# The first eight modulation parts in places of their own, and the filter network of layer 0 in another order

## The chip, the cores and the metric

The kernel runs on one NeuronCore of one Trainium2 chip. Five engines work beside each other and meet at semaphores: TensorE (matmuls, and the loads of their stationary operand), VectorE, ScalarE, GpSimd, and SyncE (SP), which here only issues DMAs. The metric is the device time of one execution in microseconds; smaller is better.

## What is computed

Two layers of a backbone over 256 latent tokens and 256 context tokens, width 1024, in float32. Cut to what the change touches:

```
for i in range(2):
    mod_l = split(silu(c)     @ w_mod[i] + b_mod[i], 6)       # w_mod[i]: 1024 x 6144
    mod_c = split(silu(c_ctx) @ w_mod[i] + b_mod[i], 6)
    uc = modulated_norm(xc, norm1_w, mod_c[0], mod_c[1]) @ w_in[i]
    ul = modulated_norm(xl, norm1_w, mod_l[0], mod_l[1]) @ w_in[i]
    ...                                                        # SSD, Hyena, mLSTM mixers, then 32 experts

modulated_norm(x, w, shift, scale) = rmsnorm(x, w) * (1 + scale) + shift

def hyena_filters(L, p):                                       # depends on weights alone
    hdn = sin(freq * (feats @ w1 + b1))
    hdn = sin(freq * (hdn @ w2 + b2))
    return (hdn @ w3).reshape(L, 2, 2, 256) * exp(-t * abs(decay))

def bidir_long_conv(z, h_fwd, h_bwd):
    two_sided = [h_fwd, 0, reversed h_bwd[1:]]
    two_sided = two_sided / sum(abs(two_sided))                # the "tap sum", one value per channel
    return irfft(rfft(z) * rfft(two_sided))
```

The input projection needs the modulated norm, and that needs vectors 0 (shift) and 1 (scale) of the modulation, each 1024 wide: the first 2048 columns of `w_mod`. The filter's spectra are needed later, in the Hyena mixer.

## The kernel before

**Modulation parts.** `w_mod` is taken in parts of 256 columns, 1 MB each in float32. Parts 0 to 3 give vector 0, parts 4 to 7 vector 1. Part n is loaded by `modulation(0, n)` on SP into one of the four slots of `ring` (2048 columns each), in rows of a kilobyte; TensorE multiplies it in eight matmuls of 256 columns that are spread over the four 32-column groups of the array; ScalarE copies the product to `grow` (`mod_rows`). When a vector's four parts are there, TensorE adds up the groups and turns the result into columns (`mod_vector`, 16 matmuls with `four`), and VectorE adds the bias (`mod_columns`). With eight parts and four slots, parts 4 to 7 wait until parts 0 to 3 are used.

**Filter network** (`filter_step`, one function on each of TensorE, ScalarE and VectorE). Step 0 and 1: a hidden layer each; VectorE brings the argument of the sine into range, ScalarE does the sine. Step 2: the taps, four matmuls of 512 columns, times the decay window. Step 3: ScalarE writes the absolute values to `tabs_v` (parts of `xbc` and `hyT`), TensorE sums them over the rows by 16 matmuls with one column each (`tapsum`), then VectorE makes sum and difference of the two directions (with a copy of each difference) and the reciprocal. Step 4: five spectra, two matmuls of 512 columns each, copied to `hfilt` by VectorE.

**Order at the start.** Each engine runs its instructions in the order of the code, and the order is written out by hand, per engine: lines 399 to 432 for SP, 614 to 648 for TensorE, 1243 to 1275 for ScalarE, 1564 to 1688 for VectorE. SP's queue is filled in this order: condition vectors, parts 0 and 1, filter parameters, parts 2 and 3, x, the DFT tables, biases and norm weights, parts 4 to 7, the layer's parameters and other constants, then the projection's weights alternating with further parts. TensorE ends the stretch with 32 transposes of the normed x; ScalarE (context) and VectorE (latent) write them to `hT` with the modulation applied; `stage_end` is a meeting of TensorE, ScalarE and VectorE. The input projection follows.

**Layer 1** has the same filter network. Its steps are placed between the experts of layer 0, at the items in `FILTER_ITEMS`; item j's three weight matrices stream through eight slots of 1 MB.

**Names.** Every matmul is recorded at line 533, every ScalarE instruction at 1208, VectorE's at 1540 to 1550, by helpers. A float32 matmul stands in the trace as two passes, so 8 matmuls are x16 (a transpose is one). PSUM has eight banks in turn (`product`).

## Time and profile before

| | us |
|---|---|
| median of 3 runs | 1513.99 |
| lowest and highest of them | 1511.68, 1515.15 |
| the profiled execution | 1514.76 |
| its span, on which all times of the trace lie | 1512.8 |
| TensorE busy in the span | 1242.1 (82%) |
| VectorE, ScalarE busy | 633.8, 315.8 |
| HBM traffic over the span | 226 GB/s |

Times of rows are in microseconds from the start of the span unless marked ns. A row of a timeline is: start, length, engine, line, operation, what is written `<-` what is read, shapes, count, and in brackets how long the engine was idle before it and what ended that idle time. "PEclk" is the clock that the throttle granted to TensorE, 1.00 being 2.4 GHz and 0.50 being 1.2 GHz. The execution of 1514.76 us is the one that the trace shows; the time of a changed kernel is compared with the median.

### The profile page before, as it was taken

How to read it: one execution, taken by the hardware profiler on the slowest of the kernel's cores; microseconds unless marked ns; L12 is line 12 of the kernel's file. 1: busy time of each engine (PE TensorE's matmuls, PEld its weight loads, DVE VectorE, ACT ScalarE, POOL GpSimd, SP SyncE). 2: the span in 40 equal slices, each digit the busy share in tenths (PEclk: the TensorE clock that was granted, in tenths of full speed). 3: DMA queues.
4: the chain of work that ended last, by engine and by line, in shares of the span. 5: the costliest groups of instructions: out<-in, count | busy, mean ns of one | idle time of the engine just before them, and what ended most of it. 6: DMA issues, size and time to landing. Idle time of an engine off the chain costs nothing. (4 is left out here: it accounts for less than half of the span.)

```text
span 1512.8 us, 20013 instructions
## 1 busy us (share of the span) xinstructions
PE 1242.1 (82%) x7740; PEld 830.7 (55%) x7740; DVE 633.8 (42%) x1275; ACT 315.8 (21%) x622; POOL 128.2 (8%) x144
## 2 busy tenths in 40 slices
PE   5899999998889668899868449999879488888880
PEld 1544548987668544555434246568767355454450
DVE  4424862055792542333212164844474522222223
ACT  3202112243333201131101122122522111111111
POOL 0000000000000011212111000000000111211210
PEclk9999999998999779998979779999989599899896
DMA  9633232244430539999989455341532489999982
GB/s 284 190 112 112 74 101 70 91 148 135 137 115 29 195 124 375 396 365 363 378 285 388 177 192 186 112 125 43 195 117 73 183 323 393 376 386 376 375 334 88
DMA packets 157910, 322.19 MB, mean 213 GB/s; under 512 B 27963, under 2 KB 117112, under 8 KB 141176
## 3 DMA queue, kind: packets, MB, share of 16 engines
q1 hardware_dynamic: 146424, 305.12, 56.6%
q0 software_dynamic: 11392, 15.77, 3.3%
q8 instruction: 64, 1.05, 0.3%
q14 instruction: 30, 0.25, 0.0%
HBM read 321.11 MB, written 21.23 MB: 226 GB/s over the span
## 5 line engine op out<-in xcount | busy, mean ns | idle before, releaser
L533 PE MATMUL bank<-hT,ring 128*128 128x512 f32 (+1 forms) x544 | 203.6, 531 | 3.8 <-DVEq L1126 3.8
L533 PE MATMUL bank<-ring,qkT 128*64 128x256 f32 x1024 | 169.1, 426 | 38.0 <-DMA ring<-in_moe_w_up 26.5
L533 PE MATMUL bank<-ring,hT 128*128 128x256 f32 (+1 forms) x928 | 179.5, 348 | 2.4 <-DVE big L1544 1.5
L1544 DVE TENSOR_TENSOR xbc<-xbc,bank 64x256 f32<-64x256 f32 x65 | 27.5, 423 | 330.1 <-ACT xbc L1208 273.9
L533 PEld LDWEIGHTS bank<-ring,hT 128*128 128x128 f32 x928 | 154.0, 193 | 21.1 <-issue 3.3
L533 PEld LDWEIGHTS bank<-hT,ring 128*128 128x128 f32 x544 | 102.4, 190 | 99.3 <-issue 93.0
L533 PEld LDWEIGHTS bank<-ring,qkT 128*64 128x64 f32 x1024 | 107.1, 153 | 72.5 <-issue 34.9
L533 PE MATMUL bank<-hT,qkT 128*64 128x256 f32 x512 | 105.4, 440 | 28.9 <-DMA hT<-in_moe_w_up 19.9
L1141 POOL DMA_INDIRECT pair_rows<-hyT,zotok x65 | 60.1, 924 | 450.9 <-DVE xbc L1550 435.5
L1208 ACT ACTIVATE xbc<-bank 64x256 f32<-64x256 f32 x65 | 24.6, 378 | 312.0 <-PE bank L533 307.7
L533 PEld LDWEIGHTS bank<-hT,qkT 128*64 128x64 f32 x512 | 62.5, 159 | 47.3 <-issue 29.0
L533 PE MATMUL bank<-xtok,qkT 128*64 128x256 f32 x272 | 75.6, 441 | 11.8 <-DMA zotok<-in_moe_w_up 9.8
L533 PE MATMUL bank<-zotok,qkT 128*64 128x256 f32 x272 | 72.9, 429 | 6.3 <-DMA ring<-in_moe_w_up 5.7
L1208 ACT ACTIVATE hyT<-bank,zotok 64x512 f32<-64x512 f32 x65 | 44.3, 682 | 161.2 <-PE bank L533 156.0
L1541 DVE TENSOR_SCALAR hyT<-bank,zotok 64x512 f32<-64x512 f32 x65 | 49.1, 755 | 64.7 <-PE bank L533 60.2
L533 PE MATMUL bank<-ring,condp 128*32 128x256 f32 x768 | 56.8, 430 | 16.8 <-DMA ring<-in_w_mod 16.8
L1136 POOL DMA_INDIRECT big<-h_rows,zotok x65 | 62.3, 959 | 55.0 <-DVE ktok L1541 35.8
L533 PE MATMUL bank<-ring,xbc 128*64 128x512 f32 x264 | 65.6, 619 | 1.1 <-DVE xbc L1550 1.1
L1208 ACT ACT_TABLE_LOAD x31 | 39.8, 1283 | 120.9 <-PE bank L533 78.4
L1544 DVE TENSOR_TENSOR big<-big,bank 128x384 f32<-128x384 f32 x48 | 26.6, 554 | 83.9 <-PE bank L533 75.7
L1150 POOL DMA_DIRECT2D grow<-in_b_mod x4 | 2.3, 579 | 691.0 <-ACT grow L1208 454.6
L1023 PEld LDWEIGHTS bank<-ident,big 64*128 64x128 f32 x520 | 38.3, 142 | 39.6 <-issue 32.6
(285 smaller groups left out, 1719.8 us busy)
## 6 DMA issues: line engine op xcount, KB each, us to landing
ring<-in_w_mod SPq DMA_DIRECT2D x48, 1024.0 KB
ring<-in_moe_w_down SPq DMA_DIRECT2D x33, 1024.0 KB
ring<-in_moe_w_gate SPq DMA_DIRECT2D x32, 1024.0 KB
ring<-in_moe_w_up SPq DMA_DIRECT2D x32, 1024.0 KB
ring<-in_w_in SPq DMA_DIRECT2D x22, 1024.0 KB
hT<-in_moe_w_gate SPq DMA_DIRECT2D x16, 1024.0 KB
hT<-in_moe_w_up SPq DMA_DIRECT2D x16, 1024.0 KB
hT<-in_moe_w_down SPq DMA_DIRECT2D x16, 1024.0 KB
```

The lines of the kernel that those rows point to most:

```text
L533: return nc.tensor.matmul(o, a, b, start=s, stop=e, **k)
L1023: last = nc.tensor.transpose(b[:, k * R:(k + 1) * R], rows_v[0:R, j % 4, k * P:(k + 1) * P], ident[0:R, 0:R])
L1136: return nc.gpsimd.indirect_dma_start(dst, None, h2_rows, bass.IndirectOffsetOnAxis(at_, 0), bounds_check=NT * P - 1, oob_is_err=False)
L1141: return nc.gpsimd.indirect_dma_start(pair_rows, bass.IndirectOffsetOnAxis(at_, 0), src, None, bounds_check=MOST_PAIRS - 1, oob_is_err=False)
L1150: pool.dma_start(modrow(m)[2:3, :], A["b_mod"][l:l + 1, m * D:(m + 1) * D]).then_inc(gate_bias_in[l][n], tick(f"gate_bias{l}{n}_in", ("gat ...
L1208: step(nc.scalar.activation(o, i, f, **k), *names)
L1541: V.tensor_scalar(o, a, s1, None, op0), *names)
L1544: step(V.tensor_tensor(o, a, b, op), *names)
```

## The change

**Loads.** The first eight parts of layer 0 no longer pass through the ring one by one. Parts 0 and 1, 2 and 3, 4 and 5 are loaded as pairs of 2 MB, in rows of two kilobytes, into ring slots 0 and 1, ring slots 2 and 3, and `hT`; parts 6 and 7 are loaded singly into parts of `xtok` and `zotok`. None of these loads waits for a slot. SP's order is now: condition vectors, filter parameters, pair 0, x, pairs 1 and 2, the DFT tables, part 6, biases and norm weights, part 7, the projection's first weight, the layer's parameters, and the other constants behind the second weight.

**Filter network.** Step 3 is split. TensorE first sums each of the four [128 x 512] blocks of absolute values over the rows, each in one column group of 32 (`tap rows`); VectorE copies the result to `ysum`; a new step 4 adds the four groups by four one-column matmuls with `four`. The sums and differences no longer wait for the tap sum; the copies of the differences are gone, and the spectra read them in `tabs_v`. The spectra are step 5. In layer 1 the steps stand at items 8, 10, 12, 14, 15 and 17.

**Order.** TensorE, ScalarE and VectorE take the first hidden layer ahead of parts 0 and 1 and the taps ahead of parts 2 and 3; ScalarE takes parts 2 and 3 and the absolute values ahead of the Sqrt of the norm; the fifth spectrum stands behind the transposes. VectorE's memsets of `vaug`, `sst` and `cst` move between filter steps, that of `hT` is dropped. In layer 0 the meeting `norm1` is replaced by TensorE's wait for the two writers of `hT`.

```
-FILTER_ITEMS = (8, 10, 12, 15, 17)
+FILTER_ITEMS = (8, 10, 12, 14, 15, 17)
...
+        pair_v = [a.rearrange("p (k n) -> p k n", k=KB) for a in (ring[:, 0:4096], ring[:, 4096:8192], hT[:, :])]
+        def first_mod(n):
+            if n < 6:
+                return pair_v[n // 2][:, :, 256 * (n % 2):256 * (n % 2) + 256]
+            return slot_v(n, KB)
...
+            def first_pair(n):
+                wm, s = A["w_mod"][0].rearrange("(p k) n -> p k n", k=KB), (0, 2, 4)[n]
+                with nc.allow_non_contiguous_dma(reason="rows of two kilobytes"):
+                    sp.dma_start(pair_v[n], wm[:, :, 512 * n:512 * n + 512]).then_inc(
+                        slot_in[s], tick(f"slot{s}_in", ("load", ("mod", 0, 2 * n)), ("load", ("mod", 0, 2 * n + 1)), by=16))
...
+            def first_single(n):
...
                     fetch("cond_in", ident[:, :], A["const_ident"])
-                    for n in MOD_FIRST[0:2]:
-                        modulation(0, n)
                     filter_parameters(0)
-                    for n in MOD_FIRST[2:SLOTS]:
-                        modulation(0, n)
+                    first_pair(0)
                     fetch("x_in", x_v[:, 0:2, :], A["ctx"][0].rearrange("(t p) d -> p t d", p=P))
...
+                    first_pair(1)
+                    first_pair(2)
                     for name, t in (("dftc", dftc), ("dfts", dfts), ("dftn", dftn)):
                         fetch("dft_in", t[:, :], A["const_" + name])
+                    first_single(6)
...
                     norm_weights(0)
-                    for n in MOD_FIRST[SLOTS:]:
-                        modulation(0, n)
-                    parameters(0)
...
+                    first_single(7)
...
                         weight((name, l, q), win[:, :, c0 + 256 * q:c0 + 256 * q + w], KB)
+                        if (l, name, q) == (0, "hy", 0):
+                            parameters(0)
...
@@ TensorE, filter_step
+                    b = product(("tap rows", l))
+                    pe.wait_ge(*due(("tabs", l)))
+                    for g in range(4):
+                        last = mm(b[32 * g:32 * g + 32, :], ones[:, 0:32], tabs_v[g // 2][:, g % 2, :, :])
+                    last.then_inc(pe_done, made(("tap rows", l)))
+                elif n == 4:
                     b = product(("tapsum", l))
-                    pe.wait_ge(*due(("tabs", l)))
-                    for o in range(2):
-                        for c in range(2):
...
+                    pe.wait_ge(*due(("tap rows in", l)))
+                    for i in range(4):
+                        last = mm(b[:, i:i + 1], ysum[:, P * i:P * i + P], four[:, 0:1])
                     last.then_inc(pe_done, made(("tapsum", l)))
...
@@ ScalarE, in the first layer's square_sums
+                    if l == 0:
+                        mod_rows(l, 2)
+                        mod_rows(l, 3)
+                        filter_step(l, 3)
                     act.wait_ge(*due(("rinv", l, n)))
                     fn(small[:, 4:8], small[:, 4:8], ACT.Sqrt, ("rstd", l, n))
...
@@ VectorE, filter_step
-                    dve.wait_ge(*due(("tabs", l)))
-                    dve.wait_ge(*due(("made", ("tapsum", l))))
+                    dve.wait_ge(*due(("made", ("tap rows", l))))
+                    copy(ysum[:, 0:512], bank(("tap rows", l))[:, :], ("read", ("tap rows", l)), ("tap rows in", l))
                     for t in range(2):
                         tt(tabs_v[t][:, 0], taps_v[:, t, 0], taps_v[:, t, 1], SUB)
-                        tt(taps_v[:, t, 0], taps_v[:, t, 0], taps_v[:, t, 1], ADD)
-                        copy(taps_v[:, t, 1], tabs_v[t][:, 0], ("tapsd", l))
+                        tt(taps_v[:, t, 0], taps_v[:, t, 0], taps_v[:, t, 1], ADD, ("tapsd", l))
+                elif n == 4:
```

TensorE's queue at the start of the program, before. `ring,condp` x8 is one part, `feats,w` and `ysum,w` are the hidden layers, `ktok,ysum` the taps, `four,grow` a vector, `ones,xbc` and `ones,hyT` the one-column tap sums:

```order
L533 MATMUL bank<-ring,condp 32x256 x16
L533 MATMUL bank<-feats,w 64x256
L533 MATMUL bank<-ring,condp 32x256 x8
L533 MATMUL bank<-ysum,w 64x256
L533 MATMUL bank<-ring,condp 32x256 x8
L533 MATMUL bank<-ktok,ysum 128x512 x4
L533 MATMUL bank<-ring,condp 32x256 x16
L533 MATMUL bank<-four,grow 64x2 x16
L533 MATMUL bank<-ones,xbc 128x1 x2
```

And now (`xbc,ones`, `hyT,ones` are the tap rows, `four,ysum` the tap sum):

```order
L558 MATMUL bank<-feats,w 64x256
L558 MATMUL bank<-ring,condp 32x256 x16
L558 MATMUL bank<-ysum,w 64x256
L558 MATMUL bank<-ktok,ysum 128x512 x4
L558 MATMUL bank<-ring,condp 32x256 x16
L558 MATMUL bank<-four,grow 64x2 x16
L558 MATMUL bank<-xbc,ones 32x512 x2
L558 MATMUL bank<-hyT,ones 32x512 x2
L558 MATMUL bank<-hT,condp 32x256 x16
L558 MATMUL bank<-four,ysum 128x1 x4
```

Both hidden layers and the taps stand one part, or two, earlier, and what were sixteen one-column matmuls are eight, in two groups around parts 4 and 5.

The same queue further on, before, from the spectra (`dftc`, `dfts`, `dftn`) over the transposes (`ident,big`) to the projection (`hT,ring`):

```order
L533 MATMUL bank<-ring,condp 32x256 x8
L533 MATMUL bank<-qkT,dftc 128x512 x4
L533 MATMUL bank<-qkT,dfts 128x512 x4
L533 MATMUL bank<-qkT,dftn 128x512 x2
L533 MATMUL bank<-ring,condp 32x256 x8
L533 MATMUL bank<-four,grow 64x2 x16
L643 MATMUL bank<-ident,big 128x128 x32
L634 MATMUL bank<-ident,prow 128x78
L533 MATMUL bank<-hT,ring 128x512 x16
```

And now:

```order
L558 MATMUL bank<-qkT,dftc 128x512 x4
L558 MATMUL bank<-xbc,dfts 128x512
L558 MATMUL bank<-hyT,dfts 128x512
L558 MATMUL bank<-xtok,condp 32x256 x8
L558 MATMUL bank<-zotok,condp 32x256 x8
L558 MATMUL bank<-xbc,dfts 128x512
L558 MATMUL bank<-hyT,dfts 128x512
L558 MATMUL bank<-four,grow 64x2 x16
L671 MATMUL bank<-ident,big 128x128 x32
L558 MATMUL bank<-qkT,dftn 128x512 x2
L662 MATMUL bank<-ident,prow 128x78
L558 MATMUL bank<-hT,ring 128x512 x16
```

Parts 6 and 7 stand behind three spectra, the fourth spectrum covers ScalarE's copy of part 7, and the fifth stands behind the transposes.

VectorE's queue before, from the norm (`big<-x,small`) to the spectra's copies (`hfilt<-bank`); `modc` is the modulation's columns:

```order
L1541 TENSOR_SCALAR big<-x,small 128x1024 x4
L1544 TENSOR_TENSOR xbc<-qkT 128x512
L1544 TENSOR_TENSOR qkT<-qkT 128x512
L1550 COPY qkT<-xbc 128x512
L1544 TENSOR_TENSOR hyT<-qkT 128x512
L1544 TENSOR_TENSOR qkT<-qkT 128x512
L1550 COPY qkT<-hyT 128x512
L1624 RECIPROCAL small<-bank 128x4
L1544 TENSOR_TENSOR modc<-bank,bmod 128x16
```

And now:

```order
L1574 TENSOR_SCALAR big<-x,small 128x1024 x4
L1577 TENSOR_TENSOR modc<-bank,bmod 128x16
L1583 COPY ysum<-bank 128x512
L1577 TENSOR_TENSOR xbc<-qkT 128x512
L1577 TENSOR_TENSOR qkT<-qkT 128x512
L1577 TENSOR_TENSOR hyT<-qkT 128x512
L1577 TENSOR_TENSOR qkT<-qkT 128x512
L1652 RECIPROCAL small<-bank 128x4
```

The columns of vector 0 and the copy of the tap rows stand ahead of the sums and differences, and the two copies behind these are gone.

## Rows read from the trace of the kernel before

**Rows 1.** Busy time by stretches: length; PE, PEld, DVE, ACT, POOL; PEclk, DMA share, GB/s.
```profile
0.00:74.50 74.50, 50.60 (x289) 28.41 (x289) 35.05 (x63) 21.70 (x35) 0.20 (x4) 0.98 0.82 240
74.50:250.00 175.50, 175.42 (x670) 89.00 (x671) 88.63 (x133) 24.50 (x40) 0.00 (x0) 1.00 0.32 99
560.00:850.00 290.00, 242.91 (x1626) 136.70 (x1624) 85.46 (x159) 43.74 (x75) 56.80 (x61) 0.91 0.95 354
```

**Rows 2.** TensorE's timeline up to the projection: start, length, what, idle before and releaser.
```profile
9.56 1.94 PE L533 MATMUL bank<-ring,condp 128*32 128x256 f32 x16 [9.56 <-DMA ring<-in_w_mod]
13.85 1.94 PE L533 MATMUL bank<-ring,condp 128*32 128x256 f32 x16 [2.35 <-DMA ring<-in_w_mod]
15.71 1.11 PE L533 MATMUL bank<-feats,w 33*64 33x256 f32 x2
...
21.64 1.11 PE L533 MATMUL bank<-ysum,w 64*64 64x256 f32 x2
...
26.36 7.16 PE L533 MATMUL bank<-ktok,ysum 64*128 64x512 f32 x8 [1.70 <-ACT ysum L1208]
...
41.24 1.02 PE L533 MATMUL bank<-ones,xbc 128*128 128x1 f32 x4
...
48.16 1.93 PE L533 MATMUL bank<-ring,condp 128*32 128x256 f32 x16
52.31 5.52 PE L533 MATMUL bank<-qkT,dftc 128*128 128x512 f32 x8 [2.21 <-DVE qkT L1550]
57.66 3.60 PE L533 MATMUL bank<-qkT,dfts 128*128 128x512 f32 x8
...
62.91 1.07 PE L533 MATMUL bank<-ring,condp 128*32 128x256 f32 x16
64.63 2.09 PE L533 MATMUL bank<-four,grow 128*64 128x2 f32 x32 [0.66 <-ACT grow L1208]
66.65 5.21 PE L643 MATMUL bank<-ident,big 128*128 128x128 f32 x32
...
74.58 0.67 PE L533 MATMUL bank<-hT,ring 128*128 128x512 f32 x1 [2.65 <-DVEq L1126]
```

**Rows 3.** VectorE's timeline: the norm, the first difference, the writing of hT.
```profile
37.59 3.12 DVE L1541 TENSOR_SCALAR big<-x,small 128x1024 f32<-128x1024 f32 x4 [1.68 <-ACT small L1208]
48.37 0.69 DVE L1544 TENSOR_TENSOR xbc<-qkT 128x512 f32<-128x512 f32 x1 [7.65 <-PE bank L533]
...
67.88 6.27 DVE L1540 TENSOR_SCALAR hT<-bank,ab 128x256 f32<-128x256 f32 x8 [0.43 <-PE bank L643]
```

**Rows 4.** SP's timeline: parts 0 and 1, the last filter load, the first projection weight.
```profile
2.87 1.26 SPq L343 DMA_DIRECT2D ring<-in_w_mod  x2
...
9.76 0.59 SPq L348 DMA_DIRECT2D hfilt<-in_hy_decay  x1
...
50.32 0.55 SPq L343 DMA_DIRECT2D ring<-in_w_in  x1
```

**Rows 5.** Stretches by DMA rate (columns as in rows 1).
```profile
10.00:14.00 4.00, 1.65 (x20) 0.57 (x16) 3.16 (x1) 0.38 (x1) 0.00 (x0) 1.00 1.11 229
...
22.00:27.00 5.00, 3.30 (x19) 1.09 (x18) 3.87 (x8) 1.02 (x3) 0.00 (x0) 1.00 1.03 405
35.00:42.00 7.00, 5.81 (x64) 3.67 (x56) 3.36 (x6) 4.76 (x8) 0.00 (x0) 1.00 1.09 349
```

**Rows 6.** ScalarE's timeline: the first of the two Abs.
```profile
37.94 1.06 ACT L1208 ACTIVATE xbc<-qkT 128x1024 f32<-128x1024 f32 x1
```

**Rows 7.** Stretches behind vector 1, for the granted clock (columns as in rows 1).
```profile
66.50:69.70 3.20, 3.20 (x19) 3.19 (x19) 2.12 (x6) 1.68 (x3) 0.00 (x0) 0.50 0.72 249
69.80:72.00 2.20, 2.13 (x20) 1.93 (x18) 2.09 (x4) 1.94 (x4) 0.00 (x0) 1.00 0.00 0
```

**Rows 8.** Layer 1's tap sum among the experts: TensorE's groups, and the stretch behind.
```profile
L533 PE MATMUL bank<-ones,hyT 128*128 128x1 f32 x16 | 2.7, 276 | 0.0
...
680.00:688.00 8.00, 8.00 (x38) 4.66 (x39) 1.66 (x3) 0.68 (x1) 0.00 (x0) 0.57 0.96 345
```

More of the change, by code:

```diff
@@ L1563, in _ @@
             copy(ident16[:, :], ident[:, :])
-            step(V.memset(vaug[:, :], 1.0))
-            step(V.memset(sst[:, :], 0.0))
-            step(V.memset(cst[:, :], 0.0))
-            step(V.memset(hT[:, :], 0.0))
             def mod_columns(l, m):
```

89 lines of the change are left out of this document (50 added, 39 removed).

## The prediction

> **What bounds the kernel now.** Read the busy time by stretches first [rows 1]. From 74.5 to 250 us TensorE is busy 175.42 of 175.50 us: the input projection has no slack, so whatever makes it begin earlier comes off the end. In the 74.5 us ahead of it TensorE is busy for 50.60 us only. The change works in that stretch, and a little in the expert stage. The question is therefore when the row at 74.58 starts, and what ended last before it.
>
> TensorE's own order [rows 2] answers it backwards. The projection waits 2.65 us for VectorE, which writes hT for 6.27 us behind the transposes [rows 2, 3]. These stand behind the second vector product (64.63), that one behind part 7 (62.91) and all ten spectrum matmuls (52.31 to 62.9), and the spectra wait 2.21 us for VectorE's sums and differences, which begin at 48.37 when 16 one-column matmuls end [rows 3]. Those begin at 41.24 and give way to part 6 at 48.16. Loads end a wait only in the first half.
>
> **The start of the chain is now one load.** After the change TensorE takes: first hidden layer; parts 0, 1; second hidden layer; taps; parts 2, 3; vector 0; tap rows; parts 4, 5; tap sum; three spectra; parts 6, 7; fourth spectrum; vector 1; transposes; fifth spectrum. Parts 0 and 1 come as one 2.10 MB load, which lands at a time P. The small filter loads are issued ahead of it. In the kernel before the last of them is issued by 10.35, with 1.31 us of issue for two parts ahead of them [rows 4], so the pair is issued at 9.04. Part 0 was issued at 2.87 and used at 9.56 [rows 2, 4]: 6.7 us for 1.05 MB. At the 349 GB/s of rows of a kilobyte 3.0 us of that is data, 3.7 us fixed. The stretch with rows of four kilobytes (x) and two (the DFT tables) moves 405 GB/s [rows 5]. So P = 9.04 + 3.7 + 5.2 (at 405), plus 0.9 for the 0.79 MB of w3 and decays (2.0 us, issued 1.1 us ahead): 18.8. At 349 it is 19.9; with w3 and decays at the 229 GB/s of the stretch in which the filter loads ran, another 1.5: 21.4. I take 19.3, nearer to 405, because two-kilobyte rows are in that stretch.
>
> The Trainium skill (DMA: Bandwidth & Descriptors, Specifications) gives 512 bytes as the least transfer for line rate, so by it rows of one and two kilobytes cost alike. That would put P at 19.9 and the time 0.6 us higher; the trace speaks against it, 349 against 405 GB/s.
>
> **From P to the projection**, in us after P. Parts 0, 1 step by 1.86 each (13.85 to 15.71): 3.7. Second hidden layer to first tap matmul, with VectorE's range reduction and ScalarE's sine, 4.72 (21.64 to 26.36): 8.4. Taps 7.16: 15.6. Parts 2, 3: 19.3. ScalarE's copy of part 3, by the 0.66 us wait at 64.63: 19.95. Two Abs of 1.06 [rows 6]: 22.1. Then the Sqrt, which moves behind them: 1.68 us from VectorE's release to its next instruction [rows 3], less the 0.1 that it waited itself: 23.7. VectorE is held by that Sqrt and does xn, 3.12: 26.8; then mod_columns 0.2, the new copy of the tap rows 0.72 (by the 0.69 us instruction on 512 columns, with 0.03 between two), and four sums and differences at 0.72: 30.6. The two copies that stood among them are gone, 0.92. The spectra start at 30.75. Three take 5.35 + 1.72 (52.31 to 57.66 for two; 3.44 for the next two): 37.8. Parts 6, 7 at 1.0 each: 39.8. Fourth spectrum 1.72: 41.6. From vector 1 to the projection 9.95 (64.63 to 74.58), less 0.3 since TensorE no longer waits for pcol and the stage's end: 51.25.
>
> With P = 19.3 the projection starts at **70.55 instead of 74.58: 4.0 us earlier**. Compare the middle: spectra at 50.05 against 52.31 (2.26), three fewer matmul pairs on the way to vector 1 against one more part (1.5), the end 0.3.
>
> **What is hidden, and by what.** The tap rows (four matmuls of 512 columns in four column groups; as many columns in all as a part's eight of 256, so 1.9 us) and parts 4, 5 run from 22.1 to 27.9 while VectorE does xn; without that cover they would cost 5.6. The tap sum, now four one-column matmuls, takes a quarter of 6.92 (41.24 to 48.16), 1.7, from 27.9 to 29.6, under VectorE's sums. The squares of x stand ahead of parts 2, 3 on ScalarE. In the kernel before VectorE has used them by 35.91 (37.59 less its wait of 1.68), 9.55 us behind the taps' start; that is 18.0 here, ahead of part 3's 19.3. The memsets moved between the filter's steps (vaug, sst, cst) lie in waits for the pair and for the taps; that of hT is dropped, and was in a wait. The fifth spectrum moves behind the transposes: those end 2.7 us before the projection starts, and it takes 1.7. Later loads: pair 1 is due at 15.6 (34.9 us), pair 2 at 24, part 7 at 38.8 (58.1). Bytes up to part 7 are 12.1 MB; at 360 GB/s from 9.5, with 1.3 to land and 2 allowed for b_mod's short rows, that is 46.4: 12 us of cover. SP's parameter loads move behind it and behind the first projection weight. The kernel before has issued all of that by 50.3 [rows 4]; even ten microseconds later they land ahead of 66, before TensorE transposes them near 70. The later weights then find ring slots free, as before, and are needed 14 us into the projection.
>
> **The expert stage.** There half of the 16 one-column matmuls take 2.7 us of busy time, all 5.3, and behind them the clock is 0.57 from 680 to 688 [rows 8]. Their successors cost about 1.0 + 1.1 at the higher level. But from 560 to 850 the DMA engines are 0.95 busy and TensorE only 242.91 of 290 us [rows 1]. Between nothing and 4 us (all of the matmuls' gain and the slow stretch's); in 680 to 688 the rate was 345 against 354 GB/s on average, so nearer to nothing: **0.5 us**.
>
> **Sum**: the profiled execution took 1514.76 us, its span 1512.8; the median is 1513.99. 4.0 + 0.5 = 4.5 less: **1509.5 us** against the median (1510.3 against the profiled one).
>
> **Rivals.**
> (A) TensorE is fast before the spectra. The first pair of spectra takes 5.35 us, the next 3.44; the taps take 0.89 us a pass, double. The profile grants 1.00 there, but the durations are those of the lower level, 1.2 GHz. After the change full-array work (tap rows, parts 4, 5) fills 5.8 us ahead of the spectra; if that raises the clock to 2.4 GHz, 1.9 more is saved: 1507.6. Against: the tap matmuls, 7 us on end, did not.
> (B) The pair lands 2 to 4 us later, since everything hangs on it one to one; P at 22.3 gives 1512.5. For: 229 GB/s in the stretch with the filter loads.
> (C) The clock falls to 0.50 behind vector 1, as from 66.5 to 69.7, and this time stays there. The fifth spectrum would cost 3.6 and end 1.4 us after hT, and the projection would lose some 1.9 until it is fast, as the spectra did: 3.3 less gained, 1512.8. Against: the clock is back at 1.00 from 69.8, when TensorE had done nothing but transposes since 66.65 [rows 7]. The Trainium skill (TensorE: Matmul & The Clock Gate, Part 4: PE-mode transpose) says that transposes do not count as TensorE's activity for the clock; by that rule this rival would be the rule, and the trace disagrees.
> (D) Slower: the whole queue moves at the rate of the stretch with small loads. At 229 GB/s 12.1 MB need 52.8 us, part 7 lands at 63.6, and 12.4 us later (part 7, spectrum, tail) the projection starts at 76.0: 1514.9. It decides from 233 GB/s down; below 220 it is over 0.2% slower, at 215 it gives 1518.4. Against: 349 and 405 in the long stretches.
> (E) The expert stage returns all of the 4 us. For: TensorE was busy throughout 680 to 688 [rows 8]. It gives 1506.
>
> **How the numbers follow.** Forecast 0.45 (its own range 1508 to 1511), A 0.12, B 0.17, C 0.10, D 0.06, E 0.10. About 0.2% (3.0 us) is what can be told from no change: 1511.0 is the bound. Faster: 0.42 of the forecast, A, E, a little of B: 0.66. Same: the rest of B and of the forecast, C: 0.28. Slower: D, 0.06. The range takes in E in part and C: 1505.5 to 1513.5.
>
> **What would show it.** Right: parts 0 and 1 start between 18.8 and 20; taps 8.4 later; VectorE idle until ScalarE's Sqrt near 43; spectra near 50; vector 1 near 61; projection near 70.5, with no wait for a load after the first pair. Wrong: a wait for a load at part 2 or later; spectra before 48 or after 52; a projection that starts at passes of 0.89 us; a fifth spectrum that ends after hT; an expert stage shorter by over 1.5 us.

## The result

The changed kernel takes 1502.38 us (median of 22 runs, 1498.19 to 1513.74) against 1513.7 us for the kernel before on the same chip (22 runs); the ratio of the two, by which kernels are compared here, is 0.994, with a 95% interval of 0.9921 to 0.996. That is 9.1 us gained (6 to 12), where 4.5 were forecast: the sign was right, the size was half of what it should have been, and the median lies below the range. The profiled execution of the changed kernel has a span of 1499.0 us against 1512.8.

### The profile page after: what moved, and what is told of

Read it like the earlier page. It is cut to its first block and busy times, and to the rows that moved or that the text cites. A ratio compares the mean times of both kernels' runs of the same rounds, so it can differ in the third digit from the quotient of the medians.

```text
span 1499.0 us, 19940 instructions
## 1 busy us (share of the span) xinstructions
PE 1222.2 (82%) x7708; PEld 818.1 (55%) x7708; DVE 629.8 (42%) x1272; ACT 315.6 (21%) x622; POOL 128.1 (9%) x144
## 5 line engine op out<-in xcount | busy, mean ns | idle before, releaser
L1577 DVE TENSOR_TENSOR xbc<-xbc,bank 64x256 f32<-64x256 f32 x65 | 27.5, 423 | 331.0 <-ACT xbc L1240 292.8
L558 PE MATMUL bank<-hT,qkT 128*64 128x256 f32 x512 | 101.0, 420 | 27.1 <-DMA hT<-in_moe_w_up 14.9
L558 PE MATMUL bank<-zotok,qkT 128*64 128x256 f32 x272 | 76.8, 446 | 10.0 <-DMA ring<-in_moe_w_up 7.6
L1240 ACT ACT_TABLE_LOAD x31 | 39.8, 1283 | 115.7 <-PE bank L558 74.1
L1055 PEld LDWEIGHTS bank<-ident,big 64*128 64x128 f32 x520 | 37.9, 141 | 39.3 <-issue 32.3
L1240 ACT ACTIVATE big<-bank,hyT 128x128 f32<-128x128 f32 x144 | 52.9, 367 | 20.6 <-PE bank L558 16.4
## 6 DMA issues: line engine op xcount, KB each, us to landing
ring<-in_moe_w_up SPq DMA_DIRECT2D x32, 1024.0 KB, 10.3
```

Source lines behind the costliest of these rows:

```text
L558: return nc.tensor.matmul(o, a, b, start=s, stop=e, **k)
L1055: last = nc.tensor.transpose(b[:, k * R:(k + 1) * R], rows_v[0:R, j % 4, k * P:(k + 1) * P], ident[0:R, 0:R])
L1240: step(nc.scalar.activation(o, i, f, **k), *names)
L1577: step(V.tensor_tensor(o, a, b, op), *names)
```

## The profile after

TensorE's timeline up to the projection (start, length, what, idle before and releaser) answers to [rows 2]:

```profile
8.12 1.08 PE L558 MATMUL bank<-feats,w 33*64 33x256 f32 x2 [8.12 <-DMA tcol<-in_const_tcol]
19.30 3.43 PE L558 MATMUL bank<-ring,condp 128*32 128x256 f32 x32 [10.10 <-DMA ring<-in_w_mod]
22.66 0.64 PE L558 MATMUL bank<-ysum,w 64*64 64x256 f32 x2
26.91 7.16 PE L558 MATMUL bank<-ktok,ysum 64*128 64x512 f32 x8 [3.61 <-ACT ysum L1240]
34.01 2.91 PE L558 MATMUL bank<-ring,condp 128*32 128x256 f32 x32
37.58 2.09 PE L558 MATMUL bank<-four,grow 128*64 128x2 f32 x32 [0.67 <-ACT grow L1240]
...
41.43 2.63 PE L558 MATMUL bank<-hT,condp 128*32 128x256 f32 x32
45.44 1.07 PE L558 MATMUL bank<-four,ysum 128*128 128x1 f32 x8 [1.38 <-DVE ysum L1583]
48.34 6.03 PE L558 MATMUL bank<-qkT,dftc 128*128 128x512 f32 x8 [1.83 <-DVE qkT L1577]
...
59.80 2.09 PE L558 MATMUL bank<-four,grow 128*64 128x2 f32 x32
61.82 4.49 PE L671 MATMUL bank<-ident,big 128*128 128x128 f32 x32
66.14 1.88 PE L558 MATMUL bank<-qkT,dftn 128*128 128x512 f32 x4
...
68.88 1.53 PE L558 MATMUL bank<-hT,ring 128*128 128x512 f32 x3 [0.79 <-issue]
```

The pair is used at 19.30, and no line after it waits for a load. The projection starts at 68.88 instead of 74.58.

Stretches of the changed kernel (length; PE, PEld, DVE, ACT, POOL busy; PEclk, DMA share, GB/s) answer to [rows 1, 7, 8]:

```profile
0.00:68.80 68.80, 42.21 (x273) 21.74 (x273) 30.47 (x59) 21.70 (x35) 0.20 (x4) 0.85 0.83 260
68.90:250.00 181.10, 181.10 (x689) 93.80 (x690) 92.52 (x140) 24.49 (x40) 0.00 (x0) 0.99 0.31 96
48.30:54.20 5.90, 5.86 (x8) 2.57 (x9) 0.80 (x2) 0.00 (x0) 0.00 (x0) 0.59 0.64 60
61.70:66.00 4.30, 4.21 (x35) 3.81 (x34) 3.72 (x8) 3.13 (x6) 0.00 (x0) 1.00 1.07 354
391.20:399.20 8.00, 7.07 (x83) 5.47 (x82) 7.48 (x16) 1.38 (x4) 0.00 (x0) 1.00 0.05 12
554.11:839.85 285.74, 236.57 (x1595) 132.96 (x1591) 84.16 (x155) 44.25 (x76) 57.77 (x62) 0.92 0.96 356
668.00:676.00 8.00, 8.00 (x68) 4.92 (x66) 2.34 (x5) 1.06 (x2) 0.93 (x1) 1.00 1.02 380
```

The projection is as dense as before. Behind vector 1 the clock is 1.00 from the start, where [rows 7] had 0.50 first, but it is 0.59 under the first spectra. Behind layer 1's new tap sum it is 1.00 (668 to 676), where [rows 8] had 0.57.

How fast the pair came in, answering to [rows 5]: from 11 to 16 us nearly all of the traffic is the pair, in rows of two kilobytes; from 17 to 20 nearly all is x, in rows of four:

```profile
11.00:16.00 5.00, 0.00 (x0) 0.00 (x0) 2.45 (x4) 0.42 (x1) 0.00 (x0) 1.00 0.99 345
17.00:20.00 3.00, 0.69 (x8) 0.40 (x12) 0.00 (x0) 0.00 (x0) 0.00 (x0) 1.00 1.02 406
```

VectorE's norm, first difference and hT, answering to [rows 3], and SP's issue of pair 0 and of the first projection weight, answering to [rows 4]:

```profile
41.23 3.12 DVE L1574 TENSOR_SCALAR big<-x,small 128x1024 f32<-128x1024 f32 x4 [4.77 <-ACT small L1240]
...
45.32 0.69 DVE L1577 TENSOR_TENSOR xbc<-qkT 128x512 f32<-128x512 f32 x1
...
62.66 6.12 DVE L1573 TENSOR_SCALAR hT<-bank,ab 128x256 f32<-128x256 f32 x8
```

```profile
7.96 0.58 SPq L417 DMA_DIRECT2D ring<-in_w_mod  x1
...
40.65 0.67 SPq L351 DMA_DIRECT2D ring<-in_w_in  x1
```

The two Abs end at 39.61 and the Sqrt behind them releases VectorE at 41.23, as the working had it. The tap sums of both layers now take TensorE 5.1 us from first to last instead of 11.4: the tap rows of `xbc` and `hyT` run at the same time in their column groups, so their two 3.0 are one 3.0, and 2.1 follow. (Before, layer 0's took 7.0 from 41.24 on, and layer 1's 4.4 from 677.79 on.)

```profile
L558 PE MATMUL bank<-xbc,ones 128*32 128x512 f32 x8 | 3.0, 829 | 0.1
L558 PE MATMUL bank<-hyT,ones 128*32 128x512 f32 x8 | 3.0, 833 | 0.0
...
L558 PE MATMUL bank<-four,ysum 128*128 128x1 f32 x16 | 2.1, 254 | 1.4 <-DVE ysum L1583 1.4
```

**Where 13.8 us between the two profiled executions went**, by markers that are the same instructions in both:

| stretch | before | after | difference |
|---|---|---|---|
| to the projection's first matmul | 74.58 | 68.88 | 5.70 |
| to GpSimd's first load of a bias row (`grow`) | 314.76 | 314.69 | 0.07 |
| between its first two | 33.48 | 30.48 | 3.00 |
| to the first scatter of layer 0's experts (`pair_rows`) | 140.57 | 140.06 | 0.51 |
| first to last scatter, "the expert stage" below | 289.90 | 285.74 | 4.16 |
| the rest | 659.51 | 659.15 | 0.36 |

The third row is neither the start nor the filter steps, and the change has no instruction there. It is taken up under the holds.

## Experiments

Each was timed beside the kernel before on the same chip, whose median was 1512.05 to 1515.28 us in four batches; the ratio is to that. "P" is where TensorE starts parts 0 and 1; in net_only, net_hold, pair_first and two_queues it waits there for the first hidden layer and not for the load. "Start" is the projection's first matmul; "stage" is the expert stage of layer 0. Each row's P, start and stage are those of one profiled execution, its ratio that of all runs.

| run | ratio, 95% interval | P | start | stage |
|---|---|---|---|---|
| before, again | 1.0004, 0.9982 to 1.0026 | 9.34 | 74.87 | 292.5 |
| changed, again | 0.9942, 0.9917 to 0.9966 | 18.11 | 68.43 | 285.9 |
| start_only | 0.9956, 0.9927 to 0.9985 | 17.97 | 67.95 | 292.4 |
| experts_only | 0.9987, 0.9963 to 1.0011 | 9.43 | 75.76 | 286.1 |
| net_only | 0.9917, 0.9891 to 0.9943 | 16.04 | 66.43 | 289.8 |
| loads_only | 1.0062, 1.0031 to 1.0093 | 18.89 | 83.02 | 289.0 |
| pair_first | 0.9915, 0.9889 to 0.9941 | 14.87 | 65.54 | 285.8 |
| two_queues | 0.9913, 0.9882 to 0.9944 | 15.28 | 65.67 | 284.4 |
| wide_sums | 0.9930, 0.9906 to 0.9955 | 21.20 | 71.03 | 284.4 |
| before_wide | 0.9998, 0.9976 to 1.0021 | 8.86 | 73.18 | 289.1 |
| narrow4 | 1.0078, 1.0052 to 1.0105 | 19.71 | 70.03 | 311.7 |
| wide4 | 0.9989, 0.9969 to 1.0009 | 20.03 | 71.31 | 298.8 |
| short_sum | 0.9931, 0.9904 to 0.9957 | 18.73 | 68.84 | 284.6 |
| no_copies | 0.9951, 0.9932 to 0.9970 | 20.02 | 71.50 | 286.4 |
| before_hold | 1.0012, 0.9991 to 1.0034 | 9.89 | 77.02 | 288.5 |
| net_hold | 0.9928, 0.9903 to 0.9952 | 15.81 | 67.83 | 284.5 |

### The two halves

start_only is the changed kernel with layer 1's filter steps as before; experts_only is the kernel before with layer 1's steps as after.

```
 # start_only: layer 1 keeps the 16 one-column matmuls
-                elif n == 3:
+                elif n == 3 and l:
...
+                                    last = mm(b[:, 2 * o + c:2 * o + c + 1], tabs_v[t][:, e, o, c * P:(c + 1) * P],
+                                              ones[:, 0:1], n == 0, n == 3)
```

> The changed kernel with layer 1's filter steps as in the kernel before (16 one-column tap sums, copies of the differences, items 8, 10, 12, 15, 17): the change at the start alone. If the start gives what its row says, 5 to 6 us below the kernel before (ratio near 0.996); if the expert stage is worth nothing (0.5 us forecast), the time is that of the changed kernel within 1 us; if it is worth its 4 us, the time is 4 us above the changed kernel.

> The kernel before with the new tap sum (rows through four column groups, four one-column matmuls, no copies, items 8, 10, 12, 14, 15, 17) in layer 1 alone, between the experts. Forecast was 0.5 us less than before; the two profiles say 4.6 us less in that stage (ratio 0.997); if TensorE's time there is covered by the loads, ratio 1.000.

By time the start gives 6.7 us (2 to 11) and layer 1's steps 2.0 (from 1.7 lost to 5.6 gained, so by time alone this half can't be told from nothing); together they are the 9 of the changed kernel. By the rows the first half is 4.85 us: the projection starts at 73.18 to 75.76 in four profiles with the old start (mean 74.60), and at 67.95 to 71.50 in eight with the new one (mean 69.75). The second is 4.5 us: the stage takes 288.5 to 292.5 in five profiles with the old filter steps (mean 290.5), and 284.4 to 289.8 in seven with the new ones (mean 286.0). So the start was forecast nearly right, and the expert stage was not.

Where in the stage the difference lies can be read more sharply. The stretch from the 13th scatter to the 16th holds the tap sum, in either form, and what follows it. Its length, and how long the granted clock stood at 0.50 in it, both in us:

| layer 1's tap sum | profile: length, at 0.50 |
|---|---|
| 16 one-column matmuls | start_only: 33.2, 13.6; before again: 32.4, 13.6; before_hold: 30.0, 6.8; loads_only: 29.3, 6.8; before: 27.0, 6.8; no_copies: 26.8, 3.4 |
| 16 matmuls of 64 columns | before_wide: 27.5, 0; wide_sums: 25.0, 0 |
| 4 one-column matmuls | short_sum: 25.3, 3.4 |
| the new form | seven profiles: 25.1 to 26.9, 3.4 in each |

The one-column form has a mean of 29.8 (30.4 in the five profiles without no_copies), the new form one of 25.8. So the 4.5 us of the whole stage arise here, and the longest of the one-column profiles are those in which the clock was low for longest.

### Network against loads

net_only is the changed kernel with the kernel before's SP queue and ring; loads_only is the other way round.

```
 # net_only, SP
-                    filter_parameters(0)
-                    first_pair(0)
+                    for n in MOD_FIRST[0:2]:
+                        modulation(0, n)
+                    filter_parameters(0)
```

> The changed kernel's filter network and order on TensorE, ScalarE and VectorE, in both layers, with the queue of loads and the ring slots of the kernel before (single parts in rows of a kilobyte, parts 0 and 1 issued first, parts 4 to 7 behind the use of parts 0 to 3). My theory (order and tap sum give the whole gain, and the pairs cost some of it, since parts 0 and 1 as one load land at 18 to 19 us and are waited for): TensorE starts parts 0 and 1 near 13.9, the taps near 25, the spectra near 46.5 to 48, the projection at 66.5 to 68.5 (changed kernel: 68.0 to 68.9), and the time is 1500.5 to 1504, that is 0 to 2 us below the changed kernel. Rival (the places of their own are what makes the order possible): parts 4 to 7, which can only be loaded when parts 0 to 3 are used, are waited for; vector 1 then stands near 64 or later, the projection starts at 72 to 75, and the time is 4 to 6 us above the changed kernel.

> The kernel before, in its own order on TensorE, ScalarE and VectorE and with its own tap sum in both layers, but with the changed kernel's queue of loads and the pairs and single parts in places of their own. My theory: slower. The second hidden layer stands behind part 2 on TensorE, and part 2 now comes with the second pair near 31 us; taps near 36, the spectra near 61, the projection at 82 to 86 (before: 74.6 to 75.8), time 1522 to 1526. Rival (the loads give part of the gain by themselves): the projection starts at 70 to 74, time 1510 to 1514.

net_only is at least as fast as the changed kernel (12.5 us gained, against 9). loads_only loses 9.4 us: its timeline shows the second pair awaited in the middle of the filter network, as foreseen.

```profile
18.89 3.64 PE L558 MATMUL bank<-ring,condp 128*32 128x256 f32 x32 [18.89 <-DMA ring<-in_w_mod]
22.46 1.10 PE L558 MATMUL bank<-feats,w 33*64 33x256 f32 x2
29.36 1.93 PE L558 MATMUL bank<-ring,condp 128*32 128x256 f32 x16 [5.80 <-DMA ring<-in_w_mod]
31.23 1.11 PE L558 MATMUL bank<-ysum,w 64*64 64x256 f32 x2
```

So the loads to places of their own give nothing by themselves, and cost 8 us in the old order. The order of the engines is the gain. In net_only no part waits for its slot: parts 4 to 7 are there when TensorE comes to them.

### What bounds the start

pair_first moves one line of the changed kernel; two_queues also takes the nine small filter loads off SP's queue.

```
 # pair_first                                   # two_queues, ScalarE
-                    filter_parameters(0)
                     first_pair(0)
+                    filter_parameters(0)       +                    act.dma_start(dst, src)   (nine times)
```

> The changed kernel with the first pair issued ahead of the ten small filter loads instead of behind them; nothing else. Theory (the landing of pair 0 bounds the start one to one): the pair lands 4 to 6 us earlier, near 13 to 14; the first hidden layer, which stands ahead of it on TensorE, then waits for its small loads and starts near 12; taps near 22 to 23, the projection at 64.0 to 65.5 (changed kernel: 68.0 to 68.9), time about 4 us below the changed kernel, 1499 to 1501. Rival (something else is next): the small filter loads behind two megabytes land so late that the first hidden layer starts after 16, or a later part is waited for; the projection then starts at 67 to 69 and the time is that of the changed kernel within 1.5 us.

> The changed kernel with the first pair issued ahead of the small filter loads, as in the run pair_first, and the nine small filter loads of layer 0 issued on ScalarE's queue instead of SP's, at the same time. Theory (two things bound the start: the landing of pair 0, and the small loads for the first hidden layer; in pair_first the latter came last, at 13.86): the first hidden layer starts at 8 to 10, the pair lands at 12 to 13.5, the taps start near 20 to 21.5, and the projection 50 us after the pair, at 62 to 63.5 (pair_first 65.5, changed kernel 68.0 to 68.9); time 2 to 3 us below pair_first, 13.5 and more below the kernel before its change. Rival (small loads beside two megabytes are slow whichever queue issues them, or a later part is waited for next): the first hidden layer still starts near 13 to 14, or a wait for a load stands at parts 2 to 7; projection at 65 to 66, time as pair_first.

TensorE in pair_first, in two_queues and in net_only:

```profile
13.86 1.08 PE L558 MATMUL bank<-feats,w 33*64 33x256 f32 x2 [13.86 <-DMA tcol<-in_const_tcol]
14.87 3.64 PE L558 MATMUL bank<-ring,condp 128*32 128x256 f32 x32
...
23.19 7.16 PE L558 MATMUL bank<-ktok,ysum 64*128 64x512 f32 x8 [3.74 <-ACT ysum L1240]
```

```profile
14.27 1.08 PE L557 MATMUL bank<-feats,w 33*64 33x256 f32 x2 [14.27 <-DMA tcol<-in_const_tcol]
...
23.60 7.16 PE L557 MATMUL bank<-ktok,ysum 64*128 64x512 f32 x8 [4.08 <-ACT ysum L1239]
```

```profile
15.03 1.08 PE L533 MATMUL bank<-feats,w 33*64 33x256 f32 x2 [15.03 <-DMA tcol<-in_const_tcol]
...
24.36 7.16 PE L533 MATMUL bank<-ktok,ysum 64*128 64x512 f32 x8 [4.08 <-ACT ysum L1215]
```

In all three the taps start 9.33 us behind the first hidden layer, and that waits for the last small load, not for the pair. The taps are thus bounded by two chains: the landing of the pair + 7.6 to 8.3 (over the eight profiles), and the first hidden layer + 9.33. Moving the pair forward gained 4.2 us on the eight-profile mean (65.54 against 69.75) and 3.9 by the two ratios' difference (0.9915 against 0.9941); then the second chain took over. two_queues tested whether SP's issue was what delayed it. It was not: the small loads were all issued by 6.51, and the last one the hidden layer needs landed at 14.27 all the same. (The hidden layer waits for seven small loads on one count. That `tcol` was the last is seen from the packets: those of 16 bytes, which are its alone, run from 9.2 to 13.7 us.)

```profile
4.40 0.88 ACTq L1243 DMA_DIRECT2D tcol<-in_const_tcol  x1
```

In the changed kernel, with nothing large ahead of it, that load was issued at 6.41 and had landed by 8.12. In two_queues the projection came at 65.67 and not at the 62 to 63.5 of the theory. pair_first and two_queues have the lowest medians of the study, 1499.46 and 1498.47 us, below both kernels compared here; between them no difference can be told, and their intervals still overlap that of the changed kernel.

### The tap sum among the experts

Four things changed there: the matmuls' own time, the clock behind them, two copies on VectorE, and the place of the step (tap rows at item 14, where the whole tap sum stood at 15). No run moves the place alone; but wide_sums and short_sum keep the old place and take no longer than the new form. wide_sums is start_only, and before_wide the kernel before, with 64 columns in each of the 16 matmuls.

```
-    last = mm(b[:, 2 * o + c:2 * o + c + 1], ..., ones[:, 0:1], n == 0, n == 3)
+    last = mm(b[:, 64 * (2 * o + c):64 * (2 * o + c) + 64], ..., ones[:, 0:64], n == 0, n == 3)
```

> The changed kernel with layer 1's filter steps as in the kernel before (the run start_only), where now each of the 16 one-column matmuls of the tap sum takes 64 columns of the ones; the count, the place and the order stay, VectorE reads every 64th column. Stage of layer 0's experts, from the first to the last scatter: 285.7 to 286.1 with the new tap sum, 289.9 to 292.5 with the 16 one-column matmuls. Theory 1 (behind one-column matmuls the granted clock falls, and the slow stretch is most of the 5.7 us): with 64 columns the clock behind them stays at 1.00 and the stage takes 286 to 288, although the matmuls themselves take as long or longer. Theory 2 (the matmuls' own 4.3 us on TensorE, each with the load of a 128-column stationary operand, and the copies on VectorE are the cost): the stage stays at 290 to 292.5.

> The kernel before with the 16 tap-sum matmuls 64 columns wide instead of one, in both layers; VectorE reads every 64th column; nothing else. Theory (behind one-column matmuls the granted clock falls; the matmuls' own time and VectorE's copies are not the cost): among the experts the 16 matmuls take 3.6 to 4.4 us with the clock at 1.00 and no slow stretch of 7 to 8 us stands right behind them; the stage from the first to the last scatter takes 284 to 288 (289.9 and 292.5 in two profiles of the kernel before); time 3 to 5 us below the kernel before. At the start the tap sum is at the lower level in either form: 6.9 us as before, projection 74 to 76. Rival (the 5.7 us of the expert stage came from the shorter work on TensorE and VectorE, and the 284.4 of wide_sums was chance): the stage stays at 289 to 293, and the time within 1.5 us of the kernel before.

The clock did as the theory said in both (the stretch behind the matmuls: start_only, then wide_sums, then before_wide):

```profile
674.00:680.00 6.00, 6.00 (x25) 2.91 (x25) 0.89 (x2) 0.21 (x1) 0.00 (x0) 0.50 0.25 102
```

```profile
671.60:680.00 8.40, 7.58 (x62) 4.72 (x63) 5.85 (x11) 1.06 (x2) 1.94 (x2) 1.00 1.01 394
```

```profile
681.00:689.00 8.00, 8.00 (x65) 4.55 (x66) 5.45 (x10) 1.06 (x2) 1.94 (x2) 1.00 0.85 326
```

A fall among or right behind the matmuls was there in every profile with 16 one-column matmuls, and with 64 of them, and in none of the others, but not always of the same length. In the kernel before, before again and start_only it begins 2.7 to 2.9 us into them and lasts 6.7 us; in no_copies, before_hold and loads_only it begins only behind them, 4.4 to 5.0 us from the first, and lasts 3.5. Here no_copies, the matmuls and what follows:

```profile
672.90:677.20 4.30, 4.30 (x44) 4.22 (x42) 0.42 (x1) 0.38 (x1) 0.00 (x0) 1.00 1.01 346
677.20:681.20 4.00, 4.00 (x13) 1.15 (x14) 1.13 (x2) 0.46 (x1) 0.00 (x0) 0.57 0.98 399
```

What decides between the two lengths stays open, and so does why the clock falls elsewhere in the stretch: in the new form for 3.4 us between tap rows and tap sum, and in start_only, before again, before_hold and loads_only a second time ahead of the matmuls, where no one-column matmul stands. The stage took 289.9 to 292.5 with the long fall and 286.4 to 289.0 with the short one.

The time followed once only: wide_sums is 4 us below start_only and its stage 8 us shorter, while before_wide takes the time of the kernel before and a stage of 289.1. With 16 matmuls the effect on the time is no larger than the scatter of this stage, so the next four runs enlarged it or took it apart. narrow4 and wide4 do the sum four times over; short_sum keeps 4 of the 16 matmuls (it leaves out the sums over three of the four blocks, so layer 1's filters are scaled wrongly); no_copies lets the spectra read the differences where they are made.

```
 # narrow4, wide4                     # no_copies
+    for again in range(4):           -    copy(taps_v[:, t, 1], tabs_v[t][:, 0], ("tapsd", l))
```

> The run start_only (changed kernel, but layer 1's filter steps as before; 1508.0, or 7.3 us below the kernel before) with the 16 one-column matmuls of layer 1's tap sum done four times over, 64 in all (17.3 us at 0.27 each, if the clock stays at 1.00). Theory 1 (their own time on TensorE is on the path, since TensorE and not the weight loads sets the end of that part of the stage): 48 more cost 13 us, and 4 or more on top where the clock falls among and behind them; time 13 to 20 us above start_only. Theory 2 (only the fall of the clock behind a one-column stretch counts): one slow stretch as before, 0 to 4 us above start_only. Theory 3 (the weight loads set the stage's pace, as forecast): 0 to 2 us above.

> The same with 64 columns in each of the 64 matmuls. Theory 1: 13 to 14 us above start_only, and as far below narrow4 as the clock's fall costs there (4 to 7 us). Theory 2: equal to start_only or 3 us below it. Theory 3: 0 to 2 us above start_only.

> The run start_only with 4 of layer 1's 16 one-column matmuls (each sum over one of its four blocks; the other twelve are left out, so layer 1's filters are scaled wrongly). Theory 1: 3.2 us less on TensorE, and no slow stretch behind: 3 to 6 us below start_only, that is the changed kernel's time (4 us below start_only) or just under it. Theory 2: 2 to 4 us below. Theory 3, and the copies as the cause: within 1 us of start_only.

> The run start_only without VectorE's two copies of the differences in layer 1 (the spectra read them where they are made), with the 16 one-column matmuls kept. The copies as the cause: 3 to 4 us below start_only. Otherwise (VectorE is busy 85 of 290 us in the stage): within 1 us of start_only.

narrow4, the first matmuls, the rest of them, and the stretch behind:

```profile
674.90:677.60 2.70, 2.70 (x26) 2.68 (x25) 0.42 (x1) 0.38 (x1) 0.00 (x0) 1.00 1.03 414
677.70:700.00 22.30, 22.30 (x106) 22.29 (x106) 0.00 (x0) 0.00 (x0) 0.00 (x0) 0.50 0.06 25
700.00:707.00 7.00, 7.00 (x38) 3.26 (x40) 2.82 (x5) 0.68 (x1) 0.62 (x1) 0.65 0.18 44
```

wide4, the matmuls and the stretch behind:

```profile
675.70:690.10 14.40, 14.40 (x130) 14.33 (x128) 0.42 (x1) 0.38 (x1) 0.00 (x0) 1.00 0.44 166
690.10:697.00 6.90, 6.90 (x58) 3.92 (x58) 4.55 (x8) 0.90 (x2) 1.94 (x2) 1.00 0.45 153
```

This settles the kind of cost. TensorE is busy without a gap in both, with as many matmuls and weight loads; with one column the clock falls to 1.2 GHz 2.7 us into them and stays there for 22.3 us and for part of the 7 behind; with 64 columns it stays at 2.4 GHz. The two ratios are 0.0089 apart, 13.5 us, and their intervals do not touch. About 10.5 of it is the matmuls themselves (25.0 us from the first to the end of the last, against 14.5), 3 what stands behind. The matmuls' own time is on the path too. wide4 has 48 wide matmuls more than wide_sums, 10.8 us of TensorE (three quarters of 14.4), and takes 8.9 us more by the ratios (0.9989 against 0.9930; their intervals allow 4 to 14). Against start_only, whose 16 carry the fall of the clock with them, it is 5.0 (0 to 10), and the 13 to 14 that Theory 1 expected did not come. So the greater part of time put on TensorE there comes out at the end, and Theory 3, by which the weight loads set the pace, is out: it had 0 to 2 for both runs. By the same share the 2.7 us of TensorE that short_sum saves (twelve of the 16 matmuls, which take 3.6 at the higher level) would be about 2, and the 1.5 that the new form saves about 1. The copies are worth 0.8 us by the ratios (0.9951 against 0.9956), which can't be told from nothing; the stage of that one profile, 286.4, speaks for more, but it is also one with the short fall.

short_sum, without the fall and with 2.7 us less on TensorE, is 3.8 us below start_only, and the changed kernel is 2.3 us below start_only (neither is clear of nothing, by the intervals). What stays open is how much of a saving as small as the fall's in the 16-matmul form reaches the end: start_only against wide_sums says 4 us, the kernel before against before_wide says nothing. In the stretch around the tap sum (the table under the two halves) before_wide's 27.5 is below the one-column form's mean of 29.8, but not below each of its profiles.

### The holds: where the clock falls in the input stage

In the third row of the table of differences the kernel before has the clock at 0.50 for 6 us and takes 3.0 us more:

```profile
397.00:405.00 8.00, 8.00 (x41) 7.15 (x41) 5.20 (x11) 0.61 (x2) 0.00 (x0) 0.57 0.00 0
```

The same instructions of the changed kernel run at 1.00 (391.20 to 399.20, above). experts_only, whose code up to there is that of the kernel before, has 30.5 us as well. Whether the moment at which the stage starts decides it was the question of two runs. before_hold and net_hold put one memset of 1.36 us ahead of the writing of hT.

```
                 modulators(0)
+                if l == 0:
+                    step(V.memset(vaug[:, :], 1.0))
```

> The kernel before with one more instruction: VectorE's memset of vaug (1.36 us, the same values again) stands between the modulation's columns and the writing of hT in layer 0, so that the projection starts some 1.4 us later, at 76.0 to 76.5. Theory (where the granted clock falls in the input stage depends on when that stage starts: profiles with the projection at 66.43, 74.58, 74.87 and 83.02 have it at 0.50 from 8 to 14 us behind GpSimd's first row, and 33.5 us between its first two rows; those at 65.54, 67.95, 68.43, 68.88, 71.03 and 75.76 have it elsewhere, and 30.5 us): 30.5 us between the two, and 3 us of the 1.4 lost come back; at the rows h1 to h4 the kernel is 1.5 to 2 us ahead of the kernel before. Rival (the two kinds belong to the code, not to the moment): 33.5 us, and every row 1.4 us later.

> The run net_only (projection at 66.43, 33.5 us between GpSimd's first two rows, expert stage 289.8 although it has the new tap sum) with the same 1.36 us memset ahead of the writing of hT. Theory (both come from the moment at which the stage starts): projection near 67.8, 30.5 us between the two rows, expert stage 285 to 287 as in the other profiles with the new tap sum; time 1 to 4 us below net_only's in spite of the hold. Rival (they belong to the code, or the ring's order of loads costs the expert stage 4 us): 33.5 us, 289 to 290, time 1.4 us above net_only's.

GpSimd's first two rows in net_only, then in net_hold (before_hold: 391.76 and 422.31, 30.55 apart, where the kernel before has 33.48 and 33.49 in two profiles):

```profile
379.51 0.70 POOL L1157 DMA_DIRECT2D grow<-in_b_mod  x1 [379.07 <-ACT grow L1215]
413.00 0.52 POOL L1157 DMA_DIRECT2D grow<-in_b_mod  x1 [32.78 <-ACT grow L1215]
```

```profile
380.85 0.70 POOL L1157 DMA_DIRECT2D grow<-in_b_mod  x1 [380.41 <-ACT grow L1215]
411.34 0.52 POOL L1157 DMA_DIRECT2D grow<-in_b_mod  x1 [29.78 <-ACT grow L1215]
```

Both profiles turned as the theory said. That the moment is the cause isn't shown, though, since other profiles differ as much without a hold. The distance between the two rows in all eighteen:

| code up to there | 30.5 | 33.4 to 33.6 | 37.9 |
|---|---|---|---|
| old order | experts_only, before_hold | before, before again, before_wide, loads_only | |
| new order | changed, changed again, start_only, wide_sums, short_sum, pair_first, net_hold | net_only, two_queues, no_copies, wide4 | narrow4 |

wide_sums, wide4 and no_copies are the changed kernel up to there, start the projection at 71.03, 71.31 and 71.50, and show 30.5, 33.6 and 33.5. The mean is 32.5 with the old order and 32.1 with the new. So the third row of the table of differences is a draw between executions and no part of the gain; what makes the draw stays open.

The times did not follow the holds. before_hold is 1.8 us above the kernel before by its ratio, net_hold 1.7 above net_only (neither can be told from nothing, and both are near the 1.4 us put in). Over many executions the start itself moves by more than a microsecond (P is 17.97 to 21.20 in eight profiles of the same start), so the median averages over such draws; a single profile doesn't. net_only's stage of 289.8, the odd one among the new ones, became 284.5 in net_hold.

## Why the prediction was wrong, point by point

Times behind P, in us; measured are the rows of the changed kernel, less 19.30.

| step | forecast | measured |
|---|---|---|
| P | 19.3 | 19.30 (mean of eight profiles 19.4) |
| taps | 8.4 | 7.61 |
| parts 2, 3 done | 19.3 | 17.6 |
| xn starts (Sqrt done) | 23.7 | 21.93 |
| spectra | 30.75 | 29.04 |
| parts 6, 7 start | 37.8 | 36.72 |
| fourth spectrum | 39.8 | 38.58 |
| vector 1 | 41.6 | 40.50 |
| projection | 51.25 | 49.58 (mean of eight profiles 50.4) |

- **Start stage.** Every step came in the order and by the mechanism forecast: one load, the Sqrt behind the Abs, the tap rows and parts 4, 5 under VectorE's work, the fifth spectrum in the shadow of hT, no later wait for a load. The term was 4.0 us and measured 4.85 over the eight profiles (5.7 in the first). The 0.9 us too little arose ahead of the spectra and is in the main TensorE's speed: in the first profile the second hidden layer took 0.64 instead of 1.11, parts 0, 1 ended 0.3 sooner, parts 2, 3 took 2.91 instead of 3.7. In the three profiles where the hidden layer took 1.11 as before (narrow4, wide4, no_copies), the spectra started 30.4 us behind P, in the other five 29.0 to 29.7. Rival A had the kind right and the place wrong: the matmuls ahead of the spectra were in part fast, and the spectra were not (6.03 us for the first two, clock 0.59).
- **P.** Right to 0.1 us in the mean, and by luck: two errors cancelled. The pair was issued at 7.96 and not at 9.04, and from its issue to P it took 11.4 us in the mean and not 10.3. The forecast took the 405 GB/s of [rows 5] for rows of two kilobytes, but three quarters of the bytes of that stretch are rows of four. The pair moved at 345 GB/s in the first profile, near the 349 of rows of a kilobyte, and x behind it, in rows of four, at 406. In the other profiles the rate from 11 to 16 us was 267 to 387, and P went with it: 17.97 and 18.11 at 381 and 387, 21.20 at 267. Rival B nearly came true in that last profile, and not in the mean.
- **Hidden costs.** Squares of x ahead of parts 2, 3, the later parameter loads, the dropped meeting: none shows on the path. SP issued the first projection weight at 40.65, ten microseconds sooner than before, and the last constant at 58.61, in time.
- **Clock behind vector 1 (rival C).** It did not come in the changed kernel: 1.00 during the transposes and the fifth spectrum (4.49 and 1.88 us). Of the twelve profiles with the new order three have the fall (narrow4, net_only, two_queues; transposes 5.46 us, mean clock 0.69), and in each the clock was back before the transposes ended, as in the kernel before. The Trainium skill (TensorE: Matmul & The Clock Gate, Part 4: PE-mode transpose) says that transposes don't count as activity for the clock, by which it should not have risen during them; [rows 7] show it rise and this trace shows it at 1.00 throughout, so both disagree.
- **Rival D.** Not seen; even the slowest landing of the pair, 267 GB/s, was above its 233, and of the runs that only reorder work loads_only alone is clearly slower, for a reason of order.
- **Expert stage: the step that failed.** The term was 0.5 us. It measured 2.3 by start_only's ratio (not clear of nothing by itself) and 4.5 by the stage's length in twelve profiles, all of it around the tap sum. The argument that failed weighs 345 GB/s behind the tap sum against 354 on average and comes to "nearer to nothing", as if the weight loads set the pace of every microsecond of the stage. wide4 and narrow4 show otherwise: of 10.8 us more put on TensorE there, 8.9 came out at the end (4 to 14), and with the lower clock 13.5 on top. How the 4 us of the real change divide is less sure: about 1 for TensorE's own time by that share, and most of the rest for the clock, which stood at 0.50 for 3.4 to 13.6 us around the one-column tap sum and for 3.4 around the new one; wide_sums and short_sum say so by their times as well, before_wide does not. Rival E named the amount and had 0.10. The 5.3 us for the 16 matmuls were misread besides: they add two groups whose rows overlap; from the first to the last it is 4.4.
- **What no sum could have.** Two profiled executions are not comparable to a microsecond: the 3.0 us of the input stage come and go between profiles of the same code. They are in the difference of the spans (13.8); start and expert stage, 4.85 and 4, already make up the 9.1 of the ratio.

The range's lower end, 1505.5, was case E with nothing more from the start than forecast. 4.85 from the start and 4 from the experts make 1505.1, just below it; by the ratio the changed kernel stands at 1504.9 on the median before (1502.0 to 1507.9), and the median of the 22 runs, 1502.38, lies at the low end of that.

## What to carry over

Where several queues meet, put the work in the order in which its inputs land, and count every input of the first instruction: here the order gave the gain and the larger loads alone cost 9 us, and when the large load was moved forward a load of 2 KB was next. A sum over partitions by many one-column matmuls on end can cost more than its own time, since the clock falls among or behind them; here it stayed up behind the sum when that was spread over column groups or given 64 columns to work on. Compare single profiles stage by stage, and take a difference of a few microseconds in a stage that the change doesn't touch for a draw between executions until several profiles say otherwise.

## What the hardware showed that was not expected

- TensorE busy without a gap fell to 1.2 GHz 2.7 us into one-column matmuls, each with the load of a 128-column operand, and stayed there for the 22.3 us that they still took; the same 64 matmuls with 64 columns ran at 2.4 GHz throughout, at 0.45 us for four passes against 0.85. With 16 of them the clock fell among or right behind them in all six profiles, for 6.7 or for 3.5 us; right behind 4 of them, or behind 16 with 64 columns, in none.
- A load of 2 KB issued at 4.40 by ScalarE, 1.5 us behind one of 2 MB on SP's queue, had landed only by 14.27; with nothing large ahead the same load took from 6.41 to 8.12. Another engine's queue didn't help: from SP, behind the same 2 MB, it was there by 13.86.
- The 2 MB pair in rows of two kilobytes moved at 345 GB/s (267 to 387 in other profiles), a load in rows of four kilobytes right behind it at 406; the landing of the pair moved between 17.97 and 21.20 us with that rate.
- Identical instructions in the input stage took 30.5, 33.5 or 37.9 us between two markers, from one profile to the next; a delay of 1.36 us turned 33.5 into 30.5 twice, but profiles without a delay differ as much.
